# Two projections of a mixing layer in three fp32r products, and a state update by head on four row groups

## What is computed

```
h = rmsnorm(x, norm1) * (1 + sc1) + sh1                  # modulation from c @ w_ada
q, f, i, g, v = split(h @ w_in)                          # 5 x 512 columns, all fp32
f = lb + (1 - lb) * sigmoid(f);  k = 1 - f               # four heads of 128
S_t = diag(f_t) S_{t-1} + k_t outer i_t;  o_t = S_t^T silu(q_t)
o = rmsnorm(o, per head) * hgrn_norm * silu(g)
y = pooling of v over windows of 2, 4, 8, 16, per-group map
x = x + g1 * (concat(o, y) @ w_out)
h2 = rmsnorm(x, norm2) * (1 + sc2) + sh2
x = x + g2 * top-4-of-32 experts(h2);  final rmsnorm     # also returned: S, last rows of v
```

## Time and profile before

| | |
|---|---|
| median of 3 runs | 2166.18 us (2164.0 to 2167.3) |
| the profiled execution | 2165.37 us, its span 2163.8 us |
| TensorE busy | 2046.5 us (95%) |
| VectorE, ACT, POOL busy | 1569.3 (73%), 1287.0 (59%), 769.2 (36%) |
| TensorE's mean granted clock | 0.972 of 2.4 GHz |
| first stage; tile loop and sample; experts | to about 191; 191 to 652; from 652 us |

### The profile page before, as it was taken

One profiled execution on the slowest core, in us unless ns is written; L12 is line 12 of the kernel. 1 busy time (PEld: TensorE's weight loads), 2 busy tenths in 40 slices (PEclk: granted clock), 3 DMA queues, 4 the chain that ended last, 5 costly groups with the idle time before them and its releaser, 6 DMA issues.

```text
span 2163.8 us, 38715 instructions
## 1 busy us (share of the span) xinstructions
PE 2046.5 (95%) x11913; PEld 1499.0 (69%) x11947; DVE 1569.3 (73%) x2132; ACT 1287.0 (59%) x1717; POOL 769.2 (36%) x997
## 2 busy tenths in 40 slices
PE   6998999999968999999999999999999999999994
PEld 4896676666646676676676668877676677788562
DVE  4533456666668687787786769988797798898657
ACT  3532344333416676676775667867676786888554
POOL 3225345555723232222242223432243243334124
PEclk8999999999968999999999999999999999999997
DMA  9767611121367788898887779999899899999765
GB/s 348 231 226 256 189 50 49 52 70 46 97 221 296 275 315 291 290 338 310 294 306 243 281 270 382 390 339 365 288 366 347 289 349 333 366 370 392 258 221 182
DMA packets 154531, 572.26 MB, mean 264 GB/s; under 512 B 22560, under 2 KB 41773, under 8 KB 120165
## 3 DMA queue, kind: packets, MB, share of 16 engines
q1 hardware_dynamic: 127405, 511.87, 62.7%
q0 software_dynamic: 25520, 56.53, 10.5%
q10 hardware_dynamic: 1552, 3.13, 0.4%
HBM read 521.36 MB, written 50.29 MB: 264 GB/s over the span
## 4 chain that ended last, share of the span: by engine, by line
PE 58%; issue 4%; ACT 4%; DVE 3%; ACTq 0%; DVEq 0%; DMA 0%; POOLq 0%
PE pg L2242 9%; PE pg L2243 9%; PE pg L2245 9%; PE py L2201 6%; PE py L2177 6%; PE py L2178 5%; PE py L2181 5%; PE pg L2215 3%; ACT hi L2378 3%; PE pt L2172 1%; PE pt L2166 1%; DVE lo L2475 1%; PE pg L2235 1%; PE pt L2187 0%; ACT L2398 0%
## 5 line engine op out<-in xcount | busy, mean ns | idle before, releaser
L2242 PE MATMUL pg<-hi,xs 128*128 128x512 f32 x1056 | 432.9, 410 | 0.0
L2243 PE MATMUL pg<-lo,xs 128*128 128x512 f32 x1056 | 412.5, 391 | 0.0
L2475 DVE TENSOR_TENSOR lo<-spare,hi 128x1024 fp32r<-128x1024 f32 x264 | 306.3, 1221 | 81.5 <-ACT hi L2378 78.6
L2475 DVE TENSOR_TENSOR lo<-w_out,hi 128x1024 fp32r<-128x1024 f32 x272 | 313.8, 1220 | 70.4 <-ACT hi L2378 69.3
L2245 PE MATMUL pg<-hi,xs 128*128 128x512 f32 x1056 | 326.1, 390 | 0.0
L2475 DVE TENSOR_TENSOR lo<-raw,hi 128x1024 fp32r<-128x1024 f32 x264 | 314.0, 1220 | 7.1
L2378 ACT ACTIVATE hi<-w_out 128x1024 fp32r<-128x1024 f32 x272 | 265.5, 1049 | 34.6 <-SPq L2009 27.2
L2378 ACT ACTIVATE hi<-spare 128x1024 fp32r<-128x1024 f32 x264 | 259.2, 1048 | 43.2 <-PE pg L2245 43.2
L2378 ACT ACTIVATE hi<-raw 128x1024 fp32r<-128x1024 f32 x264 | 270.4, 1056 | 23.3 <-PE pg L2245 23.3
L2242 PEld LDWEIGHTS pg<-hi,xs 128*128 128x128 f32 x1056 | 198.5, 188 | 71.6 <-issue 14.1
L2245 PEld LDWEIGHTS pg<-hi,xs 128*128 128x128 f32 x1056 | 198.5, 188 | 42.5
(11 more groups left out here) (486 smaller groups left out, 3571.2 us busy)
## 6 DMA issues: line engine op xcount, KB each, us to landing
w_out<-in_w_gu SPq DMA_DIRECT2D x136, 1024.0 KB, 6.9
spare<-in_w_gu SPq DMA_DIRECT2D x132, 1024.0 KB, 10.2
raw<-in_w_down SPq DMA_DIRECT2D x132, 1024.0 KB
ada_w<-in_w_ada SPq DMA_DIRECT2D x4, 2048.0 KB
spare<-in_w_ada SPq DMA_DIRECT2D x4, 2048.0 KB
moe_rows<-small SPq DMA_DIRECT2D x9, 512.0 KB, 7.0
w_v<-in_w_in SPq DMA_DIRECT2D x2, 2048.0 KB, 17.2
w_i<-in_w_in SPq DMA_DIRECT2D x2, 2048.0 KB
```

The costliest lines, as they stand in the source:

```text
L2242: pe.matmul(pg[u][b][:, :], xs[:, kt, 0, :], wh[:, u, :], start=False, stop=False)
L2243: pe.matmul(pg[u][b][:, :], xs[:, kt, 0, :], wl[:, u, :], start=False, stop=False)
L2475: dve.tensor_tensor(lo[q % RING][:, :, :], grain(q % GRAINS), hi[q % RING][:, :, :].bitcast(F32), ALU.subtract).then_inc(s["lo"], 1)
```

## The change

- `w_i` and `w_g` are split like f's and q's weights. ACT copies the high halves into the place of `spare` in tile 0: four units of i after the exponents, four units of g after the row loads (`high_in`). VectorE makes the low halves in place, over `w_i` and `w_g`, in tile 1: four single units after the copies of levels 2 to 5, two units after the last border's copy, two before the last copy (`low_in`).
- In tiles 1 to 6 hT is split too, into the places of `mul1` and `add1`: its high half by ACT after the exponent of level 3 (`high_hT`), its low half by VectorE after the copy of level 4's border step (`low_hT`). The products i and g that these tiles make for the next tile are 24 fp32r matmuls instead of eight fp32 ones (`rows_split`).
- As the originals are overwritten, `w_i` and `w_g` are loaded again in the last tile, behind f, q and hT of the sample, and the loads of f and q now come after the last g product.
- The sample's states are made by head: the keys of head m lie on partitions 32m to 32m + 31 (`columns_k_sample`), so do the masked values, and one matmul makes four sequences (512 columns) of a head. A round is four heads, on four row groups and into four banks; there are two rounds. VectorE adds a head's four sequences at a time, SP stores four sequences after each round.

The diff, cut to its core:

```diff
-        w_v, w_i, w_g = (sb(n, [P, KT, HW]) for n in ("w_v", "w_i", "w_g"))
+        with ExitStack() as split:
+            w_lo = [split.enter_context(nc.sbuf_tensor(n, [P, KT, HW], F32R)) for n in ("w_i_lo", "w_g_lo")]
+        w_i, w_g, w_v = (sb(n, [P, KT, HW]) for n in ("w_i", "w_g", "w_v"))
+        w_hi = [fq[:, 1, part, :, :] for part in range(2)]
...
-        Vz = w_g[0:NS, :, :]
+        Vz = w_g[:, 0:2, :].rearrange("p a (b v) -> p (a b) v", v=P)
...
-        state_ps = (X1, X2, X0, X1, X2, X0, X1, X2)
+        state_ps = (X1, X2, X0, L0)
+        ROUND = NB // 2
...
+            sp.wait_ge(s["g_mm"], t + 1)
             sp.dma_start(sample["f"], scratch["fqs"][0]).then_inc(s["fs_in"], 16)
             sp.dma_start(sample["q"], scratch["fqs"][1]).then_inc(s["fs_in"], 16)
-            sp.wait_ge(s["g_mm"], t + 1)
             sp.dma_start(hT[:, 0:KT * NS], scratch["hTs"]).then_inc(s["hT_in"], 16)
+            load_in(w_i, 2, "w_i_in")
+            load_in(w_g, 3, "w_g_in")
...
-                sp.wait_ge(s["S_s"], j + 1)
+                sp.wait_ge(s["S_s"], (j // ROUND + 1) * H)
...
+            def rows_split(bank, j, name):
+                for kt in range(KT):
+                    pe.matmul(bank[:, :], hT_hi[:, kt * P:(kt + 1) * P], w_hi[j][:, kt, :], start=(kt == 0), stop=False)
+                pe.wait_ge(s["w_lo"], (j + 1) * KT // 2)
+                for kt in range(KT):
+                    pe.matmul(bank[:, :], hT_hi[:, kt * P:(kt + 1) * P], w_lo[j][:, kt, :], start=False, stop=False)
+                for kt in range(KT):
+                    last = pe.matmul(bank[:, :], hT_lo[:, kt * P:(kt + 1) * P], w_hi[j][:, kt, :], start=False, stop=(kt == KT - 1))
+                last.then_inc(s[name], 1)
...
+            def states_sample(t, half):
+                if half == 0:
+                    pe.wait_ge(s["kT"], t + 1)
+                    pe.wait_ge(s["Vz"], 1)
+                    pe.wait_ge(s["vrow"], 2)
+                    pe.wait_ge(s["x1"], TILES + 1)
+                else:
+                    pe.wait_ge(s["S_s"], H)
+                for m in range(H):
+                    rows_m = slice(m * NS, (m + 1) * NS)
+                    last = pe.matmul(state_ps[m][:, :], sample["kT"][rows_m, :], Vz[rows_m, half * ROUND:(half + 1) * ROUND, :], start=True, stop=True)
+                last.then_inc(s["S_s_mm"], 1)
...
-            states_sample(u, 0, 1)
             pe.wait_ge(s["lg"], t)
             route_rows(t, P)
-            pe.wait_ge(s["vrow"], 2)
-            states_sample(u, 1, 3)
+            states_sample(u, 0)
             route_logits(t, P)
...
-            states_sample(u, 3, 5)
             pe.wait_ge(s["rank_used"], u)
             rank(u, NS, X3)
-            states_sample(u, 5, NB)
+            states_sample(u, 1)
...
+            def high_in(j):
+                for u in range(KT // 2):
+                    cut = slice(2 * u, 2 * u + 2)
+                    act.activation(w_hi[j][:, cut, :], (w_i, w_g)[j][:, cut, :], ACT.Copy).then_inc(s["w_hi"], 1)
+            def high_hT(t):
+                act.wait_ge(s["hT_in"], t * 16 + 16)
+                act.activation(hT_hi[:, :], hT[:, :], ACT.Copy).then_inc(s["hT_hi"], 1)
...
                     exps(t, P, i)
+                    if back and i == 3:
+                        high_hT(t)
...
+                if first_tile(t):
+                    high_in(0)
                 k_rows(t, P, T0)
...
                     for dst, m in adds[2:]:
                         load_row(dst, m, "rows2")
+                    high_in(1)
                 keep_v(t + 1)
...
+            def low_hT(t):
+                dve.wait_ge(s["hT_hi"], t)
+                dve.tensor_tensor(hT_lo[:, :], hT[:, :], hT_hi[:, :].bitcast(F32), ALU.subtract).then_inc(s["hT_lo"], 1)
+            def low_in(j, units):
+                dve.wait_ge(s["w_hi"], KT)
+                dve.wait_ge(s["g_mm"], 2)
+                for u in units:
+                    cut = slice(2 * u, 2 * u + 2)
+                    dve.tensor_tensor(w_lo[j][:, cut, :], (w_i, w_g)[j][:, cut, :], w_hi[j][:, cut, :].bitcast(F32), ALU.subtract).then_inc(s["w_lo"], 1)
...
+                if back == 1:
+                    between = {i: (lambda i=i: low_in(0, (i - PRE,)),) for i in range(PRE, PRE + KT // 2)}
+                    between[LV - 2] = (lambda: low_in(1, range(2)),)
+                    between[LV - 1] = (lambda: low_in(1, range(2, KT // 2)),)
...
                 if back:
-                    between[5] = (lambda: residual(t - 1, 0),)
+                    between[4] = (*between.get(4, ()), lambda: low_hT(t))
+                    between[5] = (*between.get(5, ()), lambda: residual(t - 1, 0))
...
-            add_state(0)
+            add_state(0, 0)
             logits(t, P)
             choose(t, P)
             h2_high(u, T)
-            add_state(1)
+            add_state(0, 1)
             weigh(t, P)
             place(t, P, X3)
-            add_state(2)
+            add_state(0, 2)
             logits(u, T)
             choose(u, T)
-            for j in range(3, 6):
-                add_state(j)
+            add_state(0, 3)
             weigh(u, T)
             place(u, T, X3)
-            for j in range(6, NB):
-                add_state(j)
+            for m in range(H):
+                add_state(1, m)
```

More of the change, by code:

```diff
@@ L626, in mix_sample, with columns_k_sample @@
                 last.then_inc(s["o_mm"], 1)
[L628 to L637, removed]
+            def columns_k_sample(t):
+                pe.wait_ge(s["kend"], t + 1)
+                for m in range(H):
+                    last = pe.matmul(X3[m * NS:(m + 1) * NS, 0:P], sample["kend"][:, m * NS:(m + 1) * NS], ident[:, :], start=True, stop=True)
+                last.then_inc(s["kT_ps"], 1)
+            def states_sample(t, half):
[10 more added lines that the diff above has]
+                last.then_inc(s["S_s_mm"], 1)
             def pooling(t, T):
@@ L714, in tile @@
                 pe.wait_ge(s["pool_y"], t + 1)
-                rows(X2, w_i, hT, "i_mm")
+                if first_tile(t):
+                    rows(X2, w_i, hT, "i_mm")
+                else:
+                    pe.wait_ge(s["w_hi"], KT)
+                    pe.wait_ge(s["hT_hi"], t)
+                    pe.wait_ge(s["hT_lo"], t)
+                    rows_split(X2, 0, "i_mm")
                 if back == 2:
@@ L722, in tile @@
                 pe.wait_ge(s["vx"], t + 2)
-                rows(X3, w_g, hT, "g_mm")
+                if first_tile(t):
+                    rows(X3, w_g, hT, "g_mm")
+                else:
+                    rows_split(X3, 1, "g_mm")
                 if back:
@@ L794, in _ @@
             pe.wait_ge(s["gs"], t + 1)
+            pe.wait_ge(s["w_i_in"], 48)
             project_sample(X3, w_i)
@@ L798, in _ @@
             turn(X2, "v_mm")
+            pe.wait_ge(s["w_g_in"], 32)
             project_sample(T1, w_g)
@@ L823, in _ @@
             transpose_o(t, P)
-            transpose_k(u, NS, X3)
+            columns_k_sample(u)
             pe.wait_ge(s["x1"], t)
@@ L972, in keep_i_sample @@
                 act.wait_ge(s["sam_mm"], 2)
+                act.activation(sample["v4"], X3[:, 0:P], ACT.Copy)
                 for m in range(H):
@@ L992, in k_rows @@
                 act.wait_ge(s["kT_ps"], t + 1)
-                act.activation(of(T)["kT"][0:T, :], bank[0:T, :], ACT.Copy).then_inc(s["kT"], 1)
+                act.activation(of(T)["kT"][:, :], bank[:, :] if T == P else bank[:, 0:P], ACT.Copy).then_inc(s["kT"], 1)
             def norm_o(t, T):
@@ L1330, in norm_out_sample, with add_state @@
                     dve.tensor_tensor(h2_s[:, half, :], h2_s[:, half, :], add2_s[:, half, :], ALU.add).then_inc(s["h2"], 1)
[L1332 to L1335, removed]
-                dve.tensor_tensor(rows, rows, state_ps[j][:, :], ALU.add).then_inc(s["S_s"], 1)
+            def add_state(half, m):
+                js = slice(half * ROUND, (half + 1) * ROUND)
+                dve.wait_ge(s["S_dec"], (half + 1) * ROUND)
+                dve.wait_ge(s["S_s_mm"], half + 1)
+                dve.tensor_tensor(S0[:, js, m, :], S0[:, js, m, :], state_ps[m][:, :].rearrange("p (j v) -> p j v", j=ROUND), ALU.add).then_inc(s["S_s"], 1)
             def norm_out(t, T):
@@ L1494, in _ @@
             dve.wait_ge(s["consts"], 1)
+            for m in range(1, H):
+                dve.tensor_copy(seqmask[m * NS:(m + 1) * NS, :], seqmask[0:NS, :])
             dve.memset(A[:, :], 0.0)
@@ L1854, in _ @@
             pool.wait_ge(s["v"], u + 1)
+            pool.wait_ge(s["S"], 1)
             for j in range(NB):
-                last = pool.tensor_scalar(Vz[:, j, :], sample["v"][0:NS, :], seqmask[:, j:j + 1], 0.0, ALU.mult, ALU.add)
+                last = pool.tensor_scalar(Vz[:, j, :], sample["v4"], seqmask[:, j:j + 1], 0.0, ALU.mult, ALU.add)
             last.then_inc(s["Vz"], 1)
```

19 lines of the change are left out of this document (12 added, 7 removed).

## The result

The changed kernel took 2169.64 us (median of 14 runs) beside 2165.16 us for the one before (median of 14): ratio 1.0019, 95% interval 1.0012 to 1.0026. By the forecast's bound of 0.2% that is no change, but the interval lies wholly above 1: it is slower, by 0.12 to 0.26%. One of the 14 runs took 2402.98 us at a granted clock of 0.81 (the others 0.97), and the ratio is taken without it. The forecast of 2166.3 us was 3.3 us too low; its range (2159 to 2172) held. The profiled execution took 2169.72 us with a span of 2168.1 (before: 2165.37 and 2163.8), so 4.3 us are to be found between the two traces.

The account below looks back on a forecast made before the run. TensorE, 95% busy, was taken to bound the kernel until another engine's chain ends later. Terms -16.8 + 3.2 + 8.0 + 6.2 + 0 - 0.5 = +0.1 on the median of 2166.18 gave 2166.3 us, range 2159 to 2172.

Parts of the forecast that it names:

- The products' term: Products i and g in tiles 1 to 6: twelve replaced, each 5.45 us instead of 6.85, together -16.8 us.
- Tile 0 (+3.2): ACT's eight weight copies make TensorE's state product wait 1.2 us and its g product about 2, together +3.2 us.
- Tile 1 (+8.0): VectorE's subtracts (10.4 us) and taking turns with POOL (5.5) use up its idle time; the output product waits, +8.0 us.
- the first rival: VectorE's subtracts run beside POOL without turns: tile 1 costs 2.5, five tiles 0.4 less each; 2158.8 us, chance 0.22.
- the second rival: Each turn costs the whole POOL instruction, 0.72 us: tile 1 +2.4, five later tiles +2.0; 2170.7 us, chance 0.13.
- Tiles 2 to 6 (+6.2): Waits on POOL's list transfers and hT's low half: net 1.2 us a tile in 3 to 6, 1.4 in 2.
- POOL waits for their landing before it goes on: Tiles 3 to 6: POOL waits for its list transfers, meets the shorter tile 1.95 us late; TensorE waits 0.75.
- The second wait: Tiles 2 to 6: hT's low half ahead of level 5's border makes level 6 wait 0.4 to 1.0 us.
- The last tile (0): The reloaded w_i and w_g, 2 MB each, land before TensorE wants them, and loading f and q later is covered: 0.
- The third rival: In the last tile the reloaded w_i lands after 555.2, the sample's i product waits: +4.1, 2170.4 us, chance 0.12.
- The states (-0.5): Sample's states by head: second round 2.0 us on four row groups; POOL's drain and SP at mixing's end leave -0.5.
- the 0.61 of the earlier trace: Tile 1: VectorE's extra time per POOL instruction coming between, 0.75 us alone and 1.36 beside POOL; nine taken, 5.5 us.

## Why the prediction was right, and where it was off

- **The bound and the main sum: right.** The products were the only gain, and VectorE, POOL and ACT gave it back. The products' term was mis-sized by 1.3 us: -15.5 for -16.8, since a group of eight starts slower (1.93) than the steady row has it.
- **Tile 0 (+3.2): right** in both places; +2.8 measured.
- **Tile 1 (+8.0): right** in mechanism and nearly in size; +7.1. The sizes of the first rival (no turns, 2.5) and of the second (whole instruction, 10.4) are both out here. But that the engine that comes second waits until the other's instruction is done, the second rival had right, and the price fell on the borders and on POOL's multiplies: a single subtract took 1.20. Moving four of the subtracts behind the copies gave 2.7 of it back.
- **Tiles 2 to 6 (+6.2): the sum was low, +7.7.** The step that failed is "POOL waits for their landing before it goes on". It named the right level and the right size (0.75; 0.80 measured), but VectorE's border, held from 0.38 us into POOL's last issue until the gate product was done, came last. The second wait was put at level 6 (counted from 0), 0.4 to 1.0; it is one level earlier, the sixth of the eight, 0.83, beside 0.34 to 0.5 that before had there.
- **The last tile (0): wrong, +2.3.** The forecast asked only whether w_i is there when TensorE wants it, and that was right: no wait. It did not ask what else needs the DMA engines in those 10 us. The price came through POOL's list transfers, which land twice as late beside the reload; letting POOL go on before they land took it away. The stretch is 31.4 to 33.9 in the six traces in which the lists stand beside the reload, and 29.2 in the other eight. A run of the new products without the reload was not made. The third rival looked at this reload, but at the wrong consumer.
- **The states (-0.5): right in size, by another limit.** The stretch from the rank product to the experts is 0.7 shorter. The other traces bear the sign out: the five with the old states have 48.88 to 50.29 us there, eight by head 48.15 to 48.85 (the ninth, with the weights first, 50.37). The forecast let POOL's drain end it; that is over at 651.5, and SP, held by the weights, came last at 654.9. The row groups worked at once: 2.2 us for 2.0, which came from the column groups of the earlier trace rows. The Trainium skill ("TensorE: Matmul & The Clock Gate", Part 3), from which 2.3 had been estimated, agrees with this trace (7.0 to 2.2 is 3.2 times). What the forecast had not seen is why so little is left: by head, the first store goes at 632.45 and not at 618.01 as in before, and 6 MB move at once.
- **The last tokens' routing: not in the forecast.** -5.5 and +5.4 are a stall of before's traced execution and, for the most part, the starving of one VectorE instruction; neither needs the change. That they cancel is luck. A reader of before's trace alone could have asked why TensorE's idle time there has no cause, but not what stood behind it.
- **The rule weighed.** For the turns in tile 1 the sum with the 0.61 of the earlier trace rows came nearer than the one with all of POOL's 0.72. But where POOL runs back to back, VectorE waited for eight instructions, not for one (8.45 us). The Trainium skill ("SBUF — State Buffer", Who interferes with whom) has a VectorE instruction with two SBUF inputs contend with a GpSimd instruction that reads SBUF, and calls it an exclusive lock; these eight multiplies agree with it, and cost more than one instruction would. The border also waited for the issue of a transfer and a product (2.17), which the forecast did not count as a turn.

The sum of what is measured, 0.8 - 15.5 + 2.8 + 7.1 + 7.7 + 2.3 - 5.5 + 5.4 - 0.7 = 4.4, is the 4.3 between the spans; 0.8 of it lies ahead of anything that the change touches (tile 0 starts between 189.9 and 195.3 in the fourteen traces).

## What to carry to other kernels

Splitting a product into cheaper ones paid here only once the halves were made in idle time: look for the stretch in which the helper engines have nothing due, and put the steps there, even if they look late (here the same work, moved, turned 4 us lost into 16 won, some 2 of them by a wait that the kernel before could have too). When POOL's queue gets back-to-back SBUF work, look at each two-input VectorE instruction beside it: one of them can wait for the whole run. And before a difference of a few us is given to a change, see whether TensorE's idle time without a cause is in both traces.

## What the runs showed of the hardware that was not expected

- A VectorE instruction with two SBUF inputs got no turn during eight multiplies of POOL that followed each other: 8.37 to 8.45 us in nine traces, 1.20 in four where POOL waited for it, 1.33 in before's, where one POOL multiply took 2.02.
- POOL's issue of an indirect transfer can hold such an instruction up as well. In the tile loop, borders that began 0.38 to 0.43 us into an issue took 2.12 to 2.18 us, to the end of the POOL product behind it (25 cases in six traces). Those that began 0.20 to 0.26 into it took 0.42, and the issue 1.12 to 1.19 instead of 0.96 (eight cases in eight traces). What in the issue decides it is not shown.
- Idle time of TensorE that nothing ends (9.56 us in the first expert) went to 3.82, for VectorE, when 64 increments without effect were put at the head of TensorE's program; the ratio to before went from 1.0028 to 1.0004 with it, 0.2% that is in no line of the change. Why is not shown.
